# Six norm sums over heads: one full product each, or a rounded high and a rounded low product

## The reference, cut to what matters

```python
def rms_norm_2(x, gain):
    x32 = x.astype(jnp.float32)
    y = x32 * lax.rsqrt(jnp.mean(x32 * x32, axis=-1, keepdims=True) + EPS)
    return (y * gain.astype(jnp.float32)).astype(x.dtype)
...
    km = rms_norm_2(split_heads(kv[..., :MEM_WIDTH], MEM_HEADS), k_gain)
    qm = rms_norm_2(split_heads(qm_raw, MEM_HEADS), q_gain)
...
            q = rms_norm_2(split_heads(proj[..., :MAIN_WIDTH], FOX_HEADS), fox_q_gain[j])
...
            k_sh = rms_norm_2(split_heads(kvf[..., :MAIN_WIDTH], FOX_HEADS), fox_k_gain)
```

## Time and profile before

| what | value |
|---|---|
| time, median of 3 runs | 2284.31 us (2283.43 to 2285.08) |
| the profiled execution | 2283.69 us |
| its span, first to last instruction | 2281.9 us |
| PE busy | 2270.4 us, 99% |
| weight loads on PE | 1997.4 us, 88% |
| VectorE busy | 1677.5 us, 74% |
| ScalarE busy | 1321.6 us, 58% |
| GpSimd busy | 66.3 us, 3% |
| bytes moved by DMA | 411.91 MB |

### The profile page before, as it was taken

The page is one execution under the profiler, slowest core; times in us unless marked ns, Lnnn a source line. Parts: engine busy times, 40 slices in busy tenths (PEclk is TensorE's granted clock), DMA queues, the critical chain, the costliest instruction groups (busy, mean ns, idle before and its releaser), DMA issues.

```text
span 2281.9 us, 36209 instructions
## 1 busy us (share of the span) xinstructions
PE 2270.4 (99%) x14199; PEld 1997.4 (88%) x14199; DVE 1677.5 (74%) x2130; ACT 1321.6 (58%) x1630; POOL 66.3 (3%) x104
## 2 busy tenths in 40 slices
PE   8999999999999999999999999999999999999999
PEld 7888888988888889889888888998888888889888
DVE  7876678787667666778776776688875677777773
ACT  7554567566456445675654654666654565467552
POOL 3200002000000000000000000000000000000000
PEclk9999999999999999999999999999999999999999
DMA  8655656565555555545655555534555565644653
GB/s 252 205 186 192 189 159 167 174 202 184 186 186 190 193 184 181 158 149 184 199 189 191 187 188 184 173 107 151 185 184 188 181 195 191 212 130 153 191 190 129
DMA packets 344946, 411.91 MB, mean 181 GB/s; under 512 B 7812, under 2 KB 291926, under 8 KB 344704
## 3 DMA queue, kind: packets, MB, share of 16 engines
q1 hardware_dynamic: 340432, 399.30, 54.0%
q0 software_dynamic: 4176, 10.95, 2.0%
q10 hardware_dynamic: 224, 0.07, 0.0%
HBM read 409.08 MB, written 1.21 MB: 180 GB/s over the span
## 4 chain that ended last, share of the span: by engine, by line
PE 97%; DVE 1%; DMA 1%; ACT 0%; issue 0%; SPq 0%; DVEq 0%; ACTq 0%
PE ps L605 54%; PE ps L608 27%; PE ps L633 2%; PE ps L634 1%; PE ps L635 1%; PE ps L650 1%; PE ps L652 1%; PE ps L651 1%; PE ps L902 1%; PE ps L979 1%; PE ps L980 1%; PE ps L981 1%; PE ps L931 1%; PE ps L915 1%; DMA raw<-in_w_mem_kv 0%; PE ps L1113 0%
## 5 line engine op out<-in xcount | busy, mean ns | idle before, releaser
L605 PE MATMUL ps<-h,whi 128*128 128x512 f32 x3552 | 1120.7, 396 | 0.1
L1983 DVE TENSOR_TENSOR wlo<-raw,whi 128x2048 fp32r<-128x2048 f32 x375 | 859.0, 2292 | 272.1 <-ACT whi L1340 270.9
L1340 ACT ACTIVATE whi<-raw 128x2048 fp32r<-128x2048 f32 x376 | 719.6, 1915 | 268.4 <-DMA raw<-in_ffn_w_down 157.2
L608 PEld LDWEIGHTS ps<-h,wlo 128*128 128x128 f32 x3552 | 666.3, 188 | 161.8
L608 PE MATMUL ps<-h,wlo 128*128 128x256 f32 x3552 | 702.6, 279 | 0.0
L605 PEld LDWEIGHTS ps<-h,whi 128*128 128x128 f32 x3552 | 539.1, 188 | 6.4 <-issue 5.7
L605 PE MATMUL ps<-act,whi 128*128 128x512 f32 x1408 | 444.7, 396 | 0.0
L1383 ACT ACTIVATE accT<-ps 128x512 f32<-128x512 f32 x227 | 135.4, 596 | 372.8 <-PE ps L608 372.2
L608 PEld LDWEIGHTS ps<-act,wlo 128*128 128x128 f32 x1408 | 264.7, 188 | 65.8
L608 PE MATMUL ps<-act,wlo 128*128 128x256 f32 x1408 | 278.4, 278 | 0.0
L1992 DVE TENSOR_TENSOR accT<-ps,accT 128x512 f32<-128x512 f32 x200 | 138.2, 691 | 166.3 <-ACT accT L1383 165.0
(11 more groups left out here) (407 smaller groups left out, 2329.2 us busy)
## 6 DMA issues: line engine op xcount, KB each, us to landing
raw<-in_ffn_w_gate SPq DMA_DIRECT2D x88, 1024.0 KB, 5.3
raw<-in_ffn_w_up SPq DMA_DIRECT2D x88, 1024.0 KB, 5.3
raw<-in_ffn_w_down SPq DMA_DIRECT2D x88, 1024.0 KB, 5.0
raw<-in_w_in SPq DMA_DIRECT2D x30, 1024.0 KB, 5.4
raw<-in_w_gate SPq DMA_DIRECT2D x24, 1024.0 KB, 5.4
raw<-in_w_in_a SPq DMA_DIRECT2D x13, 1024.0 KB, 5.2
raw<-in_w_branch SPq DMA_DIRECT2D x12, 1024.0 KB, 5.1
raw<-in_w_o SPq DMA_DIRECT2D x8, 1024.0 KB, 5.2
```

The costliest lines, as they stand in the source:

```text
L605: mm(dst, whi[:, r, col:col + P], rhs, start=first, stop=False, skip_group_check=True)
L608: return mm(dst[:, 0:SEQ], wlo[:, r, col:col + P], rhs[:, 0:SEQ], start=False, stop=last, skip_group_check=True)
L1340: fn(whi[:, gr % RING, :], raw[:, gr % RING, :], ACT.Copy).then_inc(hi_done, 1)
L1983: v.tensor_tensor(wlo[:, gr % RING, :], raw[:, gr % RING, :], whi[:, gr % RING, :].bitcast(F32), ALU.subtract)\
```

## The change

The six sums for memory keys, memory queries of the recurrent layer and keys of the second attention get the form of the branch stage's sub-norm. The square is needed in full and rounded; the low part is full minus rounded, also in a rounded type; PE multiplies a rounded copy of `blk` with the high and then with the low part into the same bank.

- Start: ACT squares both layers' keys at once, 1024 columns, first in full into `junk`, then rounded into `qm_r`. DVE, behind `token_taken(3, 3)`, copies `blk` into `blk_r`, waits for `mk_sq` and subtracts 1024 columns into `junk_r`, raising `mk_low`. PE waits for `mk_low` and does four rounded products in place of two full ones.
- `hgrn`: ACT's square of `hqm` is rounded. DVE, behind the write of `hqm`, copies `blk_r`, multiplies `hqm` by itself (512 columns, in full) and subtracts (`low_part`, new), raising `qn_low`.
- `kv`: ACT does each of the three squares twice, in full and rounded. DVE copies `blk_r` in slot 0 behind its split and does the three low parts in slot 2 and in slot 3, each behind the split, and at the end of slot 5.
- PE's `qk_norm` waits for `qn_low` in place of `qn_sq` where it is given a low part.
- `sq` becomes a pair of views on one buffer, fp32 and rounded, and that buffer is 8 numbers per partition longer, which moves what lies behind it by 32 bytes. The new names `sq_r`, `qn_r`, `qm_r` and `junk_r` lie on the old buffers; `blk_r` lies in the arena.

The four sums in `fox` stay as they are.

```diff
--- before.py
+++ after.py
@@ -90,6 +90,7 @@
         self.s = 0
         self.u = 0
         self.q = 0
+        self.low = 0
         self.post = 0
         self.fill = [0] * 8
         self.o = 0
@@ -234,7 +235,10 @@
         wlo = nc.alloc_sbuf_tensor_at("wlo", [P, RING, SLOT], F32R, offset=ring_base)
         whi = sb("whi", [P, RING, SLOT], F32R)
         xT = sb("xT", [P, KT, SEQ])
-        sq = sb("sq", [P, KT, SEQ])
+        sq_base = (nc.sbuf_base + 31) // 32 * 32
+        sb("squares", [P, KT * SEQ + 8])
+        sq = nc.alloc_sbuf_tensor_at("sq", [P, KT, SEQ], F32, offset=sq_base)
+        sq_r = nc.alloc_sbuf_tensor_at("sq_r", [P, KT, SEQ], F32R, offset=sq_base)
         h = sb("h", [P, KT, 2 * SEQ], F32R)
         rstd = sb("rstd", [P, SEQ + 2])
         tick = sb("tick", [P, 2])
@@ -257,6 +261,7 @@
         qn_base = (nc.sbuf_base + 31) // 32 * 32
         sb("pair", [P, 2 * SEQ + 8])
         qn = nc.alloc_sbuf_tensor_at("qn", [P, 2, SEQ], F32, offset=qn_base)
+        qn_r = nc.alloc_sbuf_tensor_at("qn_r", [P, 2, SEQ], F32R, offset=qn_base)
         hll = nc.alloc_sbuf_tensor_at("hll", [P, 2, TT, P], F32R, offset=qn_base)
         relb = sb("relb", [32, 12])
         base = nc.sbuf_base
@@ -281,12 +286,16 @@
         gmem = at("gmem", 57 * K, [P, 16])
         qm = at("qm", 64 * K, [P, DEPTH, 2, SEQ])
         junk = at("junk", 68 * K, [P, D_MODEL])
+        qm_r = at("qm_r", 64 * K, [P, DEPTH, 2, SEQ], F32R)
+        junk_r = at("junk_r", 68 * K, [P, D_MODEL], F32R)
         diag = at("diag", 72 * K, [P, 4, P])
         rstdm = at("rstdm", 74 * K, [P, SEQ])
         ssq = at("ssq", 87 * K, [P, 4])
         sqw = at("sqw", 56 * K, [P, 2, SEQ])
         rstdf = at("rstdf", 58 * K, [P, SEQ])
         onat = at("onat", 0, [P, TT, D_MODEL])
+
+        blk_r = at("blk_r", 87 * K + 512, [P, P], F32R)
 
         act = at("act", 0, [P, FT, 2 * SEQ], F32R)
 
@@ -366,6 +375,7 @@
         l_ready, p_exp, p_ready = sem("l_ready"), sem("p_exp"), sem("p_ready")
         y_hi, y_lo, mix_lo = sem("y_hi"), sem("y_lo"), sem("mix_lo")
         qn_sq, qn_rs, qn_done = sem("qn_sq"), sem("qn_rs"), sem("qn_done")
+        qn_low, mk_low = sem("qn_low"), sem("mk_low")
         f_gate, lf_done = sem("f_gate"), sem("lf_done")
         hx_ready, hs_ready = sem("hx_ready"), sem("hs_ready")
         ho_sq, ho_lo, ho_rs, ho_n = sem("ho_sq"), sem("ho_lo"), sem("ho_rs"), sem("ho_n")
@@ -724,8 +734,19 @@
                                                    src[:, i, t * P:(t + 1) * P], ident)
                 last.then_inc(filled[6], 1)
 
-            def qk_norm(src=qn, b=7):
+            def two_parts(b, high, low):
+
+                fill(b)
+                mm(ps[:, b, :], blk_r[:, :], high, start=True, stop=False)
+                mm(ps[:, b, :], blk_r[:, :], low, start=False, stop=True).then_inc(filled[b], 1)
+
+            def qk_norm(src=qn, b=7, low=None):
                 n.q += 1
+                if low is not None:
+                    n.low += 1
+                    pe.wait_ge(qn_low, n.low)
+                    two_parts(b, src[:, :, :].rearrange("p a n -> p (a n)"), low.rearrange("p a n -> p (a n)"))
+                    return
                 pe.wait_ge(qn_sq, n.q)
                 fill(b)
                 mm(ps[:, b, :], blk, src[:, :, :].rearrange("p a n -> p (a n)"), start=True, stop=True).then_inc(filled[b], 1)
@@ -810,13 +831,15 @@
                     duo(n.g, n.e, h, h_in, 6)
                     if n.f == 0:
 
-                        pe.wait_ge(mk_sq, 1)
+                        pe.wait_ge(mk_low, 1)
                         for l, b in enumerate((7, 5)):
                             fill(b)
-                            mm(ps[:, b, :], blk, qm[:, l].rearrange("p a n -> p (a n)"), start=True, stop=True).then_inc(filled[b], 1)
+                            mm(ps[:, b, :], blk_r[:, :], qm_r[:, l].rearrange("p a n -> p (a n)"), start=True, stop=False)
+                            mm(ps[:, b, :], blk_r[:, :], junk_r[:, 512 * l:512 * l + 512], start=False, stop=True)\
+                                .then_inc(filled[b], 1)
                     if arg[0] == 6:
 
-                        qk_norm(b=5)
+                        qk_norm(qn_r, 5, low=sq_r[:, 2:4, :])
 
                     def gate_totals():
 
@@ -1195,7 +1218,7 @@
                     narrow_duo(n.g, h, h_in, 6)
                     for s in range(2, 13):
                         if s == 2:
-                            qk_norm()
+                            qk_norm(qn_r, low=sq_r[:, 4:6, :])
                         hooks = {2 * p + 1: (lambda p=p: turn_at(s, p)) for p in range(3)}
                         if s in (2, 5, 8):
                             token_slot(n.g + s, n.e + s, s % 2, h, hooks)
@@ -1211,7 +1234,7 @@
                     for s in range(2, 7):
                         def between():
                             if s in (3, 5):
-                                qk_norm(qn if s == 3 else sq[:, 6:8, :])
+                                qk_norm(qn_r if s == 3 else sq_r[:, 6:8, :], low=sq_r[:, 2:4, :] if s == 3 else sq_r[:, 4:6, :])
 
                         if 3 <= s < 6:
                             token_slot(n.g + s, n.e + s, 2 * ((n.e + s) % 2), hkv, {3: between})
@@ -1407,10 +1430,12 @@
                 qk_squares(src, ready)
                 qk_roots()
 
-            def qk_squares(src, ready, dst=qn, free=0):
+            def qk_squares(src, ready, dst=qn, free=0, full=None):
                 act_e.wait_ge(*ready)
                 if n.q - free:
                     act_e.wait_ge(qn_done, n.q - free)
+                if full is not None:
+                    fn(full, src, ACT.Square)
                 fn(dst[:, :, :], src, ACT.Square).then_inc(qn_sq, 1)
                 n.q += 1
 
@@ -1492,9 +1517,10 @@
                     split(5, 5)
                     token_out(3, 2, memv[:, 1], ssq)
                     guard[1] = (acc_free, 4)
-                    fn(qm[:, 0], memk[:, 0], ACT.Square)
                     act_e.wait_ge(acc_free, 3)
-                    fn(qm[:, 1], memk[:, 1], ACT.Square).then_inc(mk_sq, 1)
+                    keys = memk[:, :, :, :].rearrange("p l a n -> p (l a n)")
+                    fn(junk[:, :], keys, ACT.Square)
+                    fn(qm_r[:, :, :, :].rearrange("p l a n -> p (l a n)"), keys, ACT.Square).then_inc(mk_sq, 1)
                     n.h = 3
                     n.n = 1
                     n.g = n.e = n.c = 4
@@ -1834,7 +1860,7 @@
                             act_e.wait_ge(drained[b], n.fill[b])
                             fn(qn[:, :, :], qn[:, :, :], ACT.Exp, scale=-0.5).then_inc(qn_rs, 1)
                         if s == 0:
-                            qk_squares(hqm[:, :, :], (summed, n.e + 1))
+                            qk_squares(hqm[:, :, :], (summed, n.e + 1), qn_r)
                         elif s < 12:
                             split(n.g + s + 3, n.g + s + 3)
                     y_upper(2)
@@ -1856,11 +1882,11 @@
                             copy_out(n.g + s, n.c + s, n.e + s, n.e + s, only=1 if s == 6 else None)
                         guard[(n.c + s) % 2] = (acc_free, n.e + s + 1)
                         if s == 1:
-                            qk_squares(fk[:, 0:2, :], (acc_free, n.e + 1))
+                            qk_squares(fk[:, 0:2, :], (acc_free, n.e + 1), qn_r, full=sq[:, 2:4, :])
                         elif s == 2:
-                            qk_squares(fk[:, 2:4, :], (acc_free, n.e + 2), sq[:, 6:8, :], 1)
+                            qk_squares(fk[:, 2:4, :], (acc_free, n.e + 2), sq_r[:, 6:8, :], 1, full=sq[:, 4:6, :])
                         elif s == 5:
-                            qk_squares(fk[:, 4:6, :], (acc_free, n.e + 3), free=1)
+                            qk_squares(fk[:, 4:6, :], (acc_free, n.e + 3), qn_r, 1, full=sq[:, 2:4, :])
                         if s >= 3:
                             norm_pair(s - 3, arg[0], n.x - 4)
                     n.g += 7
@@ -2033,6 +2059,11 @@
                     link(v.tensor_tensor(sq[:, 0:2, :], sq[:, 0:2, :], sq[:, 2 * j:2 * j + 2, :], ALU.add))
                 if j == 3:
                     v.tensor_tensor(sq[:, 0, :], sq[:, 0, :], sq[:, 1, :], ALU.add).then_inc(sum_done, 1)
+
+            def low_part(low, full, high, squares):
+
+                dve.wait_ge(qn_sq, squares)
+                v.tensor_tensor(low, full, high.bitcast(F32), ALU.subtract).then_inc(qn_low, 1)
 
             def qk_norm(dst, g_col, src=qn, b=7):
                 n.q += 1
@@ -2166,6 +2197,11 @@
                     dve.wait_ge(drained[6], 1)
                     split(5, 5)
                     token_taken(3, 3)
+                    dve.wait_ge(cst_in, 16)
+                    v.tensor_copy(blk_r[:, :], blk)
+                    dve.wait_ge(mk_sq, 1)
+                    v.tensor_tensor(junk_r[:, :], junk[:, :], qm_r[:, :, :, :].rearrange("p l a n -> p (l a n)").bitcast(F32), ALU.subtract)\
+                        .then_inc(mk_low, 1)
```

(13 more changed lines are left out.)

## The result

The changed kernel takes 2287.07 us (median), the kernel before beside it on the same chip 2283.77 us (2283.01 to 2285.08). The ratio is 1.0015, with a 95% interval of 1.0009 to 1.0021. The change makes the kernel slower by 3.3 us, and the forecast was 2.4 us faster. One of the 20 executions behind the first median took 4526.89 us, which nothing here explains; without it the median is 2287.03 us. The profiled execution of after took 2286.89 us with a span of 2285.1, against 2281.9 before.

A forecast was written before the change was run, and what follows sets the result against it. It took PE's own list, busy 99% of the span, as the bound: 0.79 us at the start plus 1.58 us at four other products gave 2.37 us off the 2284.31 us median, so 2281.9 us, range 2280.4 to 2284.4.

The forecast's parts named there:

- A: Queries' low part late, or ScalarE/VectorE stretch behind 1539 not moving with PE: part of gain lost, 2282.3 to 2283.5 us; chance 0.22.
- B: At all six sums, rounded products run at the full ones' pace: 5.2 us more, 2289.5 us; chance 0.04 together with C.
- C: Low parts uncovered, PE stops at five waits of 1.7 us: 6 us more, 2290 us; chance 0.04 together with B.
- an effect which the rows don't show: Anywhere in the kernel, an unnamed effect on the faster side by over 0.2%; chance 0.06.
- The sign that it named for short products and a long span: Recurrence stage's tail: PE's wait of 0.7 us would have grown, showing that the gain was given back there.
- the bound of 0.5 us for the queries' place: Memory queries: most that PE might lose, from an uncaused 0.54 us chain stretch less half the 0.25 us room.
- Price of the products: Six changed sums: 1.72 us becomes 0.93 at the start, 0.86 becomes 0.465 at four others; 2.37 us off PE's list.
- Memory keys: Start: added squares, copy and subtraction cost nothing; low part done near 43.2, PE wants it at 49.68.
- Memory queries: Recurrent layer: copy, square and subtraction fit VectorE's 2.14 us gap, 0.25 us of room; counted as nothing.
- Behind it VectorE's next instruction waits for PE's slot, so nothing else is late.: Behind the memory queries' low part: the added VectorE work delays no other work; no cost counted.
- Keys of the second attention: Key stage: three extra 0.63 us squares and low parts cost nothing, as pushed-back work serves PE slots over 4 us later.
- The whole 2.37 us should arrive: Kernel's end: the recurrence's late stretch starts from a PE product and weight loads move too, so all 2.37 us arrives.

The follow-up runs named there:

- the unpadded kernel: The changed kernel without the 8 numbers of padding behind the squares, all work of the change kept: 2282.18 us, ratio 0.9993.
- the one with the later key sum: The changed kernel without the padding, third key pair's squares and low part moved behind the last slot's accumulation and norm: 2281.57 us, ratio 0.9992.
- the last one: The changed kernel without padding, third key sum later, high weights, `h` and arena at remainder 64 by 128 bytes, low weights at 0: 2263.76 us, ratio 0.9915.
- the padded kernel: The kernel before with 32 bytes of padding behind the squares and nothing else: 2288.46 us, ratio 1.0021.
- the arena moved alone: The kernel before with 32 bytes of padding directly ahead of the arena, `h`, `accT` and constants staying: 2288.52 us, ratio 1.0021.
- `weights` 8 longer: The kernel before with high weights, `h` and arena all moved by 32 bytes, raw and low weights staying: 2274.08 us, ratio 0.9958.
- all at 64: The kernel before with high weights, `h` and arena at remainder 64 by 128 bytes, low weights at 0: 2265.97 us, ratio 0.9922.
- the low weights at 32: The kernel before with high weights, `h` and arena at remainder 64 by 128 bytes, raw and low weights moved, low weights at 32: 2283.1 us, ratio 0.9999.
- all at 96: The kernel before with high weights, `h` and arena at remainder 96 by 128 bytes, low weights at 0: 2284.1 us, ratio 1.0002.

## Why the prediction was wrong

**The step that failed first was one that it left out.** The change's own text says that the squares' buffer is longer "which moves what lies behind it by 32 bytes". The sum gave this no term, not even nothing with bounds. All of PE's 99% was treated as a fixed length from which products are taken. The move cost 4.9 us (2287.07 to 2282.18 without it), and 4.7 of it is the down stages. The range ended at 2284.4 for the same reason: A, B and C all look for a loss in the sums and their cover, and none in the products that the change doesn't touch. The only chance that the prediction gave to an effect which the rows don't show, 0.06, stood on the faster side. The sign that it named for short products and a long span, PE's wait of 0.7 us in the recurrence's tail growing, did not come either: that wait is 0.7 us in both kernels.

Two smaller points of the sum. It was laid on 2284.31 us, the median of three runs; 20 runs give 2283.77, so forecast and range stand 0.5 us too high. And the bound of 0.5 us for the queries' place does not follow from its own terms: 0.54 less half of 0.25 is 0.42.

**Price of the products: right.** 0.93 us for four and 0.47 for a pair, as read from the branch stage. The Trainium skill, "FP8 and Floating Point Precision", section "TensorE Precision Notes", gives four passes for a true fp32 product. By that, an estimate from the page, one rounded product would be 0.215 us of the 0.86; the trace has 0.233, and 2.37 us stays the better sum.

**Memory keys: right.** VectorE's rows in after, start and duration:

```profile
41.23 0.21 DVE L2201 CAST blk_r<-cst 128x128 fp32r<-128x128 f32 x1
...
41.37 1.21 DVE L2203 TENSOR_TENSOR junk_r<-junk,qm_r 128x1024 fp32r<-128x1024 f32 x1
```

It is done at 42.6, forecast 43.2, and PE asks at 49.34.

**Memory queries: the cover held, the gain did not stay.** VectorE, the place forecast as tight:

```profile
1464.68 0.69 DVE L2690 TENSOR_TENSOR hqm<-ps,rstd 128x512 f32<-128x512 f32 x1 [0.40 <-PE ps L645]
1465.28 0.22 DVE L2692 CAST blk_r<-cst 128x128 fp32r<-128x128 f32 x1
1465.42 0.68 DVE L2694 TENSOR_TENSOR sq<-hqm 128x512 f32<-128x512 f32 x1
1466.13 0.69 DVE L2066 TENSOR_TENSOR sq_r<-sq,qn_r 128x512 fp32r<-128x512 f32 x1
```

The low part ends at 1466.82 and PE multiplies at 1467.33, without a wait; the room is 0.5 us, twice the forecast, because the copy starts in the shadow of the instruction ahead. PE is 0.40 us ahead from there. But 22 us on it stops for `Lh`, and 0.36 to 0.40 us are gone, all that this sum had brought. The chain of after there:

```profile
1486.83 2.20 DVE wlo L2009
1489.42 0.87 DVE Lh L2611 x3
1490.34 1.09 PE ps L1190 x8
```

In before, the chain stays on PE through this stretch. VectorE's rows say why the gain is lost, after and then before:

```profile
1467.53 0.69 DVE L2690 TENSOR_TENSOR accT<-ps,rstd 128x512 f32<-128x512 f32 x1 [0.70 <-PE ps L645]
...
1489.15 1.14 DVE L2611 TENSOR_SCALAR Lh<-Lh,rinv 128x256 f32<-128x256 f32 x4
```

```profile
1487.49 1.14 DVE L2575 TENSOR_SCALAR Lh<-Lh,rinv 128x256 f32<-128x256 f32 x4
```

The run of ScalarE's and VectorE's work that ends in `Lh` starts where VectorE takes up PE's slot 1, the last product ahead of the sum (line 645, line 635 in before). From there to `Lh` it takes 21.62 us in after and 21.61 in before, where it starts at 1465.88. It hangs on a product ahead of the shortened one and so does not move with it, and PE had next to no room against it. The step that failed is "Behind it VectorE's next instruction waits for PE's slot, so nothing else is late." It asks only what gets late, and not what fails to get early. The loss of 0.4 us is in the traces of the unpadded kernel, of the one with the later key sum and of the last one too. The prediction looked for such a stretch only behind 1539, and there nothing was lost. This is rival A's mechanism at another place. It was priced at 0.4 to 0.9 us, and the size fits.

**Keys of the second attention: "cost nothing" was wrong by 0.5 us.** The first two low parts and PE's products in the stage were covered, and PE gained 0.75 us. The step that failed is "the accumulations and splits pushed back by 0.6 to 1.3 us serve slots of PE that begin over 4 us later". The last slot's accumulation, `fz`, serves a bank that PE reuses at once. VectorE and PE in before:

```profile
1819.96 0.42 DVE L2707 TENSOR_TENSOR fz<-ps,accT 128x256 f32<-128x256 f32 x1
...
1820.53 0.70 PE L605 MATMUL ps<-h,whi 128*128 128x512 f32 x2
```

`fz` ends at 1820.38 and PE's first product of feed-forward 6 starts 0.15 us later. That was all the room. The chain of after, with the extra square in it, and PE's row:

```profile
1815.94 0.47 ACT fv L1415
1816.41 0.52 ACT sq L1438
1816.92 0.52 ACT qn_r L1439
1817.44 0.79 ACT h L1389 x2
1818.24 1.82 ACT whi L1363
1820.09 2.29 DVE wlo L2009
1822.38 0.34 DVE fz L2754
1822.86 0.70 PE ps L615 x2
```

```profile
1822.86 0.70 PE L615 MATMUL ps<-h,whi 128*128 128x512 f32 x2 [0.40 <-DVE fz L2754]
```

The extra piece is ScalarE's second square, 0.52 us on the chain; VectorE's low part, from 1819.07 to 1819.75, lies beside the split's ScalarE half and costs nothing. Moving both behind the accumulation took the wait away, as the run of that shows.

**"The whole 2.37 us should arrive": wrong.** Taking off the 0.36 and the 0.52 leaves 1.5 us, and the unpadded kernel measures 1.5 (2283.7 less 2282.18). That the two agree so well is in part luck. PE has the same 14199 instructions in both kernels, so their starts can be compared one by one in the two traces. The unpadded kernel is 0.66 us ahead before the first changed product, where the change has done nothing for PE; over all kept traces this lead in the start goes from 0.7 us ahead of before to 1.4 behind. From there the six products gain 2.3 us, and PE loses 0.4 for `Lh`, 0.1 at the start of the feed-forward behind the recurrence, 0.5 for `fz` and 0.3 for `h`: 1.0 us is left. The same reading gives 1.6 us for after against the padded kernel, 2.0 with the later key sum, and 2.0 for the last kernel against its places without the sums. So 2.0 us is what the sums bring where `fz` is covered, and what lacks to 2.37 is the loss for `Lh`.

The third new wait, for `h` in the last feed-forward, hangs on a slot whose weights come by a DMA of 9.1 us. It does not need the rounded sums: kernels without them have it in the same stretch, of 0.2 to 0.5 us. They are those with the arena moved alone, with `weights` 8 longer, with all at 64, with the low weights at 32 and with all at 96. In the first of them:

```profile
PE ps L605 <- DVE h L2014: 0.2, 1, 0.2
```

Before and the kernel with the later key sum don't have it. It is a place on the edge, and what tips it is not settled.

## What to carry to other kernels

When a matrix engine is busy 99% of the time, treat a change of any buffer's size as a change to every product whose operand lies behind it: write down the start addresses before and after, and price the move, or keep the addresses fixed. Compare the spacing of repeated groups over a whole stage, since the duration of one product hides 1%. And before added work on a side engine is called free, follow its queue to the last item before a stage boundary, where a bank or buffer is taken up again within a fraction of a microsecond. A product made shorter moves forward only what starts behind it: work of other engines that starts ahead of it stays where it was, and takes the gain back where the matrix engine meets its result.

## What was unexpected of the hardware

PE's sustained pace depends on where its operands start in SBUF. Steps of 32 bytes give 693, 700, 707 and 708 ns for the same four products of 1536 columns in all, at a granted clock of 1.0 throughout, and over this kernel that is from 2293.5 us down to 2266 us with the same instructions. High weights, low weights and moving operand all take part, as far as the runs part them: `raw` moved with the low weights, `xT` and `sq` with the high ones. Neither equal remainders nor a fixed distance explains all of it, and one stage of one kernel ran at 707 ns on places that gave 693 in its other stages. The Trainium skill, "SBUF — State Buffer", section "Operand start alignment", asks only that an operand start at a multiple of its element size, and says that this is about legality; all placements here obey it and differ by 27 us. Why 64, 64 and 0 is the best of those tried stays open: no run moved one operand through all remainders with the others fixed, whether 16 or 8 byte steps matter was not tried, nor whether places 128 bytes apart are alike, and no run tells whether reads by PE collide with each other or with the other engines' accesses.
